# Opening stage of a diffusion-layer kernel: x loaded between the first weight pieces, u prepared in both halves of a period, tile bursts in two parts

## What is computed

```python
def modulation(cvec, w_ada, b_ada):
    mod = jax.nn.silu(cvec) @ w_ada + b_ada          # w_ada: 2048 x 6144
    shift, scale, gate = jnp.split(mod[:, None, :], 3, axis=-1)
    return shift, scale, gate

def mixer_layer(x, shift, scale, gate, w_in, ...):
    u = rmsnorm(x, norm_pre_w) * (1 + scale) + shift
    aq, ak, av, az, mq, mk, mv, mo, mz, mg, ga, gb = split_proj(u, w_in)   # u @ w_in
    ...      # windowed attention, mLSTM, merge
    out = rmsnorm(merged @ w_out, norm_post_w)
    return x + gate * out, ...
```

## Time and profile before

| | before |
| --- | --- |
| median of three runs | 2243.02 us (2242.98 to 2243.2) |
| the profiled execution | 2240.9 us, its span 2239.3 us |
| PE busy | 2123.8 us, 95% of the span |
| DVE, ACT, POOL busy | 868.3, 643.5, 101.5 us |
| PEclk, mean | 0.977 |
| L1377, the products behind the start stage | 66% of the chain that ended last |

### The profile page before, as it was taken

One profiled execution on the slowest core, in us unless ns is written; L12 is line 12 of the kernel. 1 busy time (PEld: TensorE's weight loads), 2 busy tenths in 40 slices (PEclk: granted clock), 3 DMA queues, 4 the chain that ended last, 5 costly groups with the idle time before them and its releaser, 6 DMA issues.

```text
span 2239.3 us, 34071 instructions
## 1 busy us (share of the span) xinstructions
PE 2123.8 (95%) x13450; PEld 1973.3 (88%) x13450; DVE 868.3 (39%) x1666; ACT 643.5 (29%) x1046; POOL 101.5 (5%) x184
## 2 busy tenths in 40 slices
PE   3889999999999999999999999999999899989995
PEld 0459999999999999999999989999999899967774
DVE  4775755432224223222322234343434433342223
ACT  4763111223223323332232222222222422221221
POOL 2001000000000000000000000000000100000000
PEclk7999999999999999999999999999999999999998
DMA  6874656542233234223422335353434534313223
GB/s 247 274 234 123 205 174 173 176 120 75 84 113 88 75 90 119 76 75 90 120 75 76 112 93 138 100 137 100 134 103 107 167 121 122 122 57 122 75 75 131
DMA packets 295166, 274.00 MB, mean 122 GB/s; under 512 B 17920, under 2 KB 243960, under 8 KB 292640
## 3 DMA queue, kind: packets, MB, share of 16 engines
q1 hardware_dynamic: 282416, 218.21, 34.0%
q0 software_dynamic: 12656, 54.40, 6.5%
HBM read 232.65 MB, written 39.92 MB: 122 GB/s over the span
## 4 chain that ended last, share of the span: by engine, by line
PE 90%; DVE 4%; issue 2%; DMA 2%; ACT 1%; SPq 1%; DVEq 0%; POOL 0%; POOLq 0%; ACTq 0%
PE bank L1377 66%; PE bank L1601 9%; PE bank L1466 2%; PE bank L1292 2%; PE bank L1348 2%; PE bank L1516 2%; PE bank L1331 1%; PE bank L1507 1%; PE bank L1518 1%; PE bank L1439 1%; DMA Y<-in_x_prompt_dram 1%; DVE XL L1249 1%; DVE WL L862 1%; DVE XL L1223 0%; PE bank L1421 0%
## 5 line engine op out<-in xcount | busy, mean ns | idle before, releaser
L1377 PE MATMUL bank<-XH,WH 128*128 128x320 f32 x3392 | 790.2, 314 | 20.2 <-POOL WORK L548 7.9
L1377 PE MATMUL bank<-XL,WH 128*128 128x320 f32 x3392 | 774.9, 310 | 0.0
L1377 PE MATMUL bank<-XH,WL 128*128 128x320 f32 x3392 | 774.7, 310 | 0.0
L844 DVE TENSOR_TENSOR WL<-RAW,WH 128x1024 fp32r<-128x1024 f32 x244 | 298.8, 1225 | 998.8 <-ACT WH L618 998.1
L618 ACT ACTIVATE WH<-RAW 128x1024 fp32r<-128x1024 f32 x244 | 258.2, 1059 | 1197.1 <-PE bank L1377 1026.5
L1377 PEld LDWEIGHTS bank<-XH,WH 128*128 128x128 f32 x3392 | 566.7, 189 | 29.7 <-issue 20.4
L1377 PEld LDWEIGHTS bank<-XL,WH 128*128 128x128 f32 x3392 | 569.6, 189 | 0.0
L1377 PEld LDWEIGHTS bank<-XH,WL 128*128 128x128 f32 x3392 | 569.0, 188 | 0.0
L1601 PE MATMUL bank<-WH,XH 128*128 128x512 f32 x320 | 130.7, 408 | 13.9 <-ACT WORK L818 5.9
L1601 PE MATMUL bank<-WH,XL 128*128 128x512 f32 x320 | 126.7, 396 | 0.0
L1601 PE MATMUL bank<-WL,XH 128*128 128x512 f32 x320 | 126.6, 396 | 0.0
(11 more groups left out here) (198 smaller groups left out, 1515.9 us busy)
## 6 DMA issues: line engine op xcount, KB each, us to landing
RAW<-in_w_in_dram SPq DMA_DIRECT2D x180, 512.0 KB, 4.9
proj_dram<-OUTS POOLq DMA_DIRECT2D x92, 320.0 KB, 3.9
WORK<-in_w_ada_dram SPq DMA_DIRECT2D x54, 512.0 KB, 4.1
RAW<-in_w_ada_dram SPq DMA_DIRECT2D x42, 512.0 KB, 4.9
RAW<-in_w_out_dram SPq DMA_DIRECT2D x32, 512.0 KB, 3.7
WORK<-proj_dram SPq DMA_DIRECT2D x20, 640.0 KB, 4.7
WORK<-proj_dram POOLq DMA_DIRECT2D x32, 320.0 KB, 3.8
RAW<-in_w_proj_a_dram SPq DMA_DIRECT2D x16, 512.0 KB, 3.9
```

Of the source, the lines that this page charges most:

```text
L844: V.tensor_tensor(WL[:, gs % 2, :], RAW[:, gs % 4, :], WH[:, gs % 2, :].bitcast(F32), ALU.subtract).then_inc(lo_done, 1)
L1377: ins = pe.matmul(banks[n][:, 0:HALF_TOK], w[:, k, :], x[:, k0 + k, n * HALF_TOK:(n + 1) * HALF_TOK], start=(first and k == 0 and wi == 0) ...
```

## The change

Three edits, all in the start stage:

1. **x between the first pieces.** SP issues piece g, then block g of x, for g = 0 to 4. Each block has a semaphore of its own. ACT squares block g right behind hi(g). DVE makes the mean ahead of lo(6) and scales one block ahead of each of lo(8) to lo(12).
2. **u over both halves.** `start_u(k)` puts the modulation of a chunk at a4, a6, b0 and b2, and so the splits at a5, a7, b1 and b3. The transposes move one piece later on PE and ACT (behind q = 3 to 7), and the copy out waits for the splits that it needs rather than for all four.
3. **Bursts in two parts.** `START_PE` is a list of its own for PE: a burst's first k-block, then the first ada piece of the next group, then the second k-block. `START_DONE[g]` is the place of piece g in PE's count of used pieces, and every wait on `start_used` goes by it. The last three bursts stay whole.

```diff
+START_PE = []
+for _g, (_kind, _j, _q) in enumerate(START):
+    if _kind == "tiles":
+        START_PE += [(_g, 0), (_g, 1)]
+    elif _q == 0 and _g and START[_g - 1][0] == "tiles":
+        START_PE.insert(len(START_PE) - 1, (_g, None))
+    else:
+        START_PE.append((_g, None))
+START_DONE = {}
+for _g, _part in START_PE:
+    if _part != 0:
+        START_DONE[_g] = len(START_DONE) + 1
...
 def start_w_free(g):
 
-    return max((p for p in range(g) if start_w(p) == start_w(g)), default=-1) + 1
+    return max((START_DONE[p] for p in range(g) if start_w(p) == start_w(g)), default=0)
...
+def start_u(k):
+
+    c, i = divmod(k, 4)
+    return start_at("ada", 2 * c + 2, 4 + 2 * i) if i < 2 else start_at("ada", 2 * c + 3, 2 * i - 4)
...
-            for g in range(4):
-                start_load(g)
             for b in range(5):
+                start_load(b)
                 src = x_sample[0, b * P:(b + 1) * P, :] if b < NB else x_prompt[0]
-                sp.dma_start(XT[:, b, :], src).then_inc(x_in, 16)
-            for g in range(4, N_START):
+                sp.dma_start(XT[:, b, :], src).then_inc(x_in[b], 16)
+            for g in range(5, N_START):
                 start_load(g)
...
                 if c:
-                    act.wait_ge(u_lo, 4 * c)
+                    act.wait_ge(u_lo, 4 * c - 3 + min(f, 3))
...
-                if g == 4:
-                    for b in range(5):
-                        act.wait_ge(x_in, 16 * 5)
-                        if b:
-                            act.wait_ge(sq_done, b)
-                        nc.scalar.activation(SQ, XT[:, b, :], ACT.Square, accum_out=SS[:, b:b + 1]).then_inc(sq_done, 1)
...
                 start_hi_part(g)
+                if g < 5:
+                    act.wait_ge(x_in[g], 16)
+                    if g:
+                        act.wait_ge(sq_done, g)
+                    nc.scalar.activation(SQ, XT[:, g, :], ACT.Square, accum_out=SS[:, g:g + 1]).then_inc(sq_done, 1)
                 for c in range(4):
                     for f in range(5):
-                        if g == start_at("ada", 2 * c + 1, 2 + f) + 2:
+                        if g == start_at("ada", 2 * c + 1, 3 + f) + 2:
                             transposed_x(c, f)
                     for i in range(4):
-                        if c < 3 and g == start_at("ada", 2 * c + 2, 4 + i):
+                        if c < 3 and g == start_u(4 * c + i):
                             modulate(c, i)
...
-                if g == 4:
+                if g == 6:
                     dve.wait_ge(sq_done, 5)
                     V.tensor_scalar(SS[:, :], SS[:, :], 1.0 / D, EPS, ALU.mult, ALU.add).then_inc(ms_done, 1)
-                if g == 5:
+                if 8 <= g < 13:
                     dve.wait_ge(rstd_done, 1)
-                    for b in range(5):
-                        V.tensor_scalar(XT[:, b, :], XT[:, b, :], RSTD[:, b:b + 1], None, ALU.mult).then_inc(xn_done, 1)
+                    b = g - 8
+                    V.tensor_scalar(XT[:, b, :], XT[:, b, :], RSTD[:, b:b + 1], None, ALU.mult).then_inc(xn_done, 1)
...
                 for k in range(12):
-                    if g == start_at("ada", 2 * (k // 4) + 2, 4 + k % 4) + 1:
+                    if g == start_u(k) + 1:
                         split_u(k)
...
-            def start_tiles(g, m):
+            def start_tiles(g, m, k):
...
-                if kt < KT - 1:
+                if k == 1 and kt < KT - 1:
                     ins.then_inc(start_used, 1)
 
             pe.wait_ge(cs_done, 1)
-            for g in range(N_START):
+            for g, part in START_PE:
                 kind, j, q = START[g]
                 if kind == "ada":
                     mod_piece(g, j, q)
                     if q == 1 and j:
                         mod_columns(j - 1)
-                    if j % 2 and 2 <= q < 7:
-                        transposed_x(j // 2, q - 2)
+                    if j % 2 and q >= 3:
+                        transposed_x(j // 2, q - 3)
                 else:
-                    start_tiles(g, j)
+                    start_tiles(g, j, part)
```

More of the change, by code:

```diff
@@ L62, in start_w_free @@
 def start_w_free(g):
-    return max((p for p in range(g) if start_w(p) == start_w(g)), default=-1) + 1
+    return max((START_DONE[p] for p in range(g) if start_w(p) == start_w(g)), default=0)
 def start_raw_count(g):
     return sum(16 if START[p][0] == "ada" else 32 for p in range(g % START_RAW, g + 1, START_RAW))
-WIDE_FREE = max(p for p in range(N_START) if start_w(p) >= 2) + 1
+WIDE_FREE = max(START_DONE[p] for p in range(N_START) if start_w(p) >= 2)
+def start_u(k):
+    c, i = divmod(k, 4)
+    return start_at("ada", 2 * c + 2, 4 + 2 * i) if i < 2 else start_at("ada", 2 * c + 3, 2 * i - 4)
 C_IDENT, C_TRIF, C_TRIB, C_SEL, C_PERM, C_BAND, C_COS, C_SIN, C_END = 0, 128, 256, 384, 392, 520, 2056, 2568, 3080
@@ L266, in hybrid_layer @@
         XT = OR
-        rows_in, const_in, x_in, aconst_in = sem("rows_in"), sem("const_in"), sem("x_in"), sem("aconst_in")
+        rows_in, const_in, x_in, aconst_in = sem("rows_in"), sem("const_in"), [sem(f"x_in{b}") for b in range(5)], sem("aconst_in")
         m0_in, mnull = sem("m0_in"), sem("mnull")
@@ L865, in mod_row @@
             def mod_row(j):
-                dve.wait_ge(start_used, start_at("ada", j, 7) + 1)
+                dve.wait_ge(start_used, START_DONE[start_at("ada", j, 7)])
                 if j:
@@ L1333, in mod_piece @@
                 ins.then_inc(start_used, 1)
-            def start_tiles(g, m):
+            def start_tiles(g, m, k):
                 pe.wait_ge(start_lo, g + 1)
                 wh, wl = start_wh[start_w(g)], start_wl[start_w(g)]
-                for k in range(2):
-                    kt = 2 * m + k
-                    if m == 5 and k == 1:
-                        mod_columns(7)
-                    pe.wait_ge(u_lo, kt + 1)
-                    for i in range(3):
-                        cs = slice(384 * k + P * i, 384 * k + P * i + P)
-                        for wi, (w, x) in enumerate(((wh, XH), (wh, XL), (wl, XH))):
-                            for n in range(2):
-                                ins = pe.matmul(bank[2 * i + n][:, 0:HALF_TOK], w[:, cs],
-                                                x[:, kt, n * HALF_TOK:(n + 1) * HALF_TOK],
-                                                start=(kt == 0 and wi == 0), stop=(kt == KT - 1 and wi == 2))
-                        if kt == KT - 1:
-                            ins.then_inc(tiles_done, 1)
-                if kt < KT - 1:
+                kt = 2 * m + k
+                if m == 5 and k == 1:
+                    mod_columns(7)
+                pe.wait_ge(u_lo, kt + 1)
+                for i in range(3):
+                    cs = slice(384 * k + P * i, 384 * k + P * i + P)
+                    for wi, (w, x) in enumerate(((wh, XH), (wh, XL), (wl, XH))):
+                        for n in range(2):
+                            ins = pe.matmul(bank[2 * i + n][:, 0:HALF_TOK], w[:, cs],
+                                            x[:, kt, n * HALF_TOK:(n + 1) * HALF_TOK],
+                                            start=(kt == 0 and wi == 0), stop=(kt == KT - 1 and wi == 2))
+                    if kt == KT - 1:
+                        ins.then_inc(tiles_done, 1)
+                if k == 1 and kt < KT - 1:
                     ins.then_inc(start_used, 1)
             pe.wait_ge(cs_done, 1)
-            for g in range(N_START):
+            for g, part in START_PE:
                 kind, j, q = START[g]
```

## The result

The changed kernel takes 2227.4 us (median of four runs, 2225.42 to 2228.63) against 2243.0 of the kernel before: a ratio of 0.9932, 95% interval 0.992 to 0.9944, 15.6 us faster. I had forecast 2233.5 with a range from 2228.5.

The account below looks back on a forecast made before the run. PE, busy 95% of the span, was taken as the bound, so the start stage had to end sooner: 9.0 + 0.95 + 1.7 - 2.55 + 0.4 = 9.5 us, from 2240.9 to 2231.4 profiled, median 2233.5; range 2228.5 to 2237.5.

Parts of the forecast that it names:

- x between the pieces: Opening: last block of x in at 25.65, lo(12) ending at 47.5 instead of 56.5, 9.0 us gained.
- The price of a scaling, 1.74: DVE in the opening: each of five scalings of x counted at 1.74 us, 8.7 together.
- Behind lo(12) the order is as before: Opening after lo(12): hi steps and copies alternate on ACT as before, so the mod_columns move by the same 9.0 us.
- Second halves: The two second halves: 1.27 us less on DVE, 0.4 lost to T1's later place, 0.85 gained twice, 1.7 us.
- First halves, the stall: The three first halves: PE stalls 0.85 us ahead of b4 behind the fourth split, 2.55 us lost in all.
- The gaps ahead of T0 get a little shorter but stay, so I keep this loss, less 0.4 in all: First halves: slow-clock losses of 1.06, 1.25 and 1.44 us stay, only 0.4 us of them gained.
- The tail: Last stretch, from 170.7 us: last three bursts whole, order kept, no gain; unchanged at 17.8 us.
- The half burst: PE in the start stage: half a burst estimated at about 2.65 us, from a first half's 17.60 less its other work.
- the third: Rival, first halves: PE stays at 1.2 GHz, up to 16.5 us more each; 2250 for one, 2283 for three; 3%.
- The first rival: Start stage: the stalls vanish, PE full throughout and no clock loss; 26 us gained, 2217; 5%.

Follow-up runs that it names:

- x only: The kernel before with the first edit alone (x between the pieces, squares and scalings spread): 2236.62 us, ratio 0.997.
- the three kernels of the table: Bursts only and the kernel before with eight or three filler matmuls in PE's gaps: 2242.63, 2255.09 and 2238.83 us.
- x and shift: The kernel before with the first edit and, of the second, only the transposes one piece later: 2233.99 us, ratio 0.9959.
- bursts only: The kernel before with the third edit alone, bursts in two parts: 2242.63 us, ratio 1.0002.
- u only: The kernel before with the second edit alone, u over both halves and transposes one piece later: 2233.88 us, ratio 0.9965.
- filler runs: The kernel before with eight or three matmuls nobody reads in each of PE's gaps ahead of a5, a6, a7 and T0: 2255.09 and 2238.83 us.
- eight-matmul filler: The kernel before with eight matmuls nobody reads in each of PE's gaps ahead of a5, a6, a7 and T0: 2255.09 us, ratio 1.0064.
- filler, three: The kernel before with three matmuls nobody reads in each of PE's gaps ahead of a5, a6, a7 and T0: 2238.83 us, ratio 0.998.
- x and u: The kernel before with the first and second edit, bursts whole: 2225.22 us, ratio 0.9924.
- u and bursts: The kernel before with the second and third edit, x loaded, squared and scaled as before: 2236.4 us, ratio 0.9972.
- late memset: The changed kernel with POOL clearing its accumulator only after all five blocks of x are scaled: 2223.32 us, ratio 0.9916.

## Why the prediction was too small

By its own steps, profiled execution against profiled execution, where the last burst starts 14.2 us earlier instead of 9.5:

- **x between the pieces**: the chain was right. x came in at 25.64 (25.65), lo(12) ended 8.7 us earlier (9.0). The price of a scaling, 1.74, was the mean of a long one and four short ones; in the changed kernel they took 4.52 and four times 1.27, 9.6 together against 8.77. That cost the forecast little, but it hid a gain that was there to be had.
- **"Behind lo(12) the order is as before"** was wrong, since the transposes stand one piece later, and the figure built on it came out near by luck. With the order really kept (x only) the second columns stand at 59.75, 6.9 us earlier and not 9.0 (7.8 against the 67.6 of the three kernels of the table that keep the old opening and the old place of the transposes): PE was at the slow clock there, for which I had nothing in the sum and up to 1 us in the range. The shift of the transposes won 1.9 back (x and shift, 57.84), and in the trace of the changed kernel the clock came back early besides: 56.88, 9.73 us earlier. Together with the stretch behind it (10.91 us from the columns to the burst, forecast some 11.1) the first burst came 10.85 us earlier instead of 9.95: 0.9 us of the miss, which is no more than the spread of the clock's return between single executions.
- **Second halves**: forecast 0.85 less, measured 0.93 and 0.91. Right, with its parts: bursts only has the 0.4 longer (0.37), u only has the 1.27 less (19.35 - 18.07 = 1.28).
- **First halves, the stall** ahead of b4: forecast 0.85, there with 0.72; the whole first half at full clock is 17.17 against the 16.66 of the filler runs, so 0.5 of it counts at the end: 1.55 us in three places instead of 2.55, 1.0 of the miss.
- **"The gaps ahead of T0 get a little shorter but stay, so I keep this loss, less 0.4 in all"**: this is the step that failed. The gaps did stay, three of four of them, but the loss didn't stay with them. I had the loss of before nearly right (1.06 + 1.25 + 1.44 = 3.75 by the windows, 3.3 by the filler runs) and kept 3.35 of it. In the changed kernel 17.41, 17.21 and 17.16 leave some 0.25 in the first burst and nothing in the others: 3.1 us of the miss, less the 0.4 by which I had the loss of before too large. The cause is shown: the edit that keeps the clock in the first halves is the second (u only, PEclk 0.99 to 1.00), not the third (bursts only, 0.92 to 0.93) and not the first (x only, 0.89 to 0.91), nor the shift of the transposes (x and shift, first halves of 18.1 to 18.2); and filling the pauses does the same with the order untouched.
- **The tail**: 17.8 before, 17.9 after, as said.
- **The half burst**: the working that I gave for 2.65 comes to 2.95. Measured it is 2.71 (85.20 to 87.91), and nothing in the sum hung on it.

These make 0.9 + 0.1 + 1.0 + 3.1 - 0.4 = 4.7, the 14.2 against 9.5. Another 1.3 us of the profiled difference (15.5) lies behind the start stage, where the two kernels have the same instructions. From the last burst to the end all traces but that of the eight-matmul filler take between 2066.6 and 2069.9 us (before 2068.6, changed 2067.4), so it lies within the spread of single executions.

Of the rivals, the third pointed the wrong way. I took "HAM oscillation — how this bites in real kernels" of the Trainium skill, "TensorE: Matmul & The Clock Gate", as a warning against parted bursts. The runs agree with the rule itself: what pauses too much loses its clock (x only), what is filled keeps it (filler, three). The page's case is a PE that waits for DMAs; here pauses of 1.0 to 1.3 us behind DVE were enough. The runs say that the parting of the bursts mattered neither way for it, and that the spread of the splits, which closes one of four pauses, was the application of the rule here. I read it for the part that looked chopped and not for the part that removed waits. The first rival (stalls vanish) came true for the clock alone, not for DVE's share: the wait of ACT for T1's place is still there with 3.77 us in the changed kernel:

```profile
91.74 1.06 ACT L661 ACTIVATE WH<-RAW 128x1024 fp32r<-128x1024 f32 x1 [3.77 <-PE bank L1365]
```

## What to carry to other kernels

Where PE waits in short pauses, look at the clock behind them: the pauses cost twice, and an edit that removes even one of four can win back the clock for work that it doesn't touch. Take the loss out of the sum as a term of its own with its own chance, and don't carry it over by habit; a few filler matmuls in the gaps measure it (3.3 us here) with nothing else changed. An edit in three parts should be run in parts: here the third cost some 1.9 us in the stage (x and u against the changed kernel, u only against u and bursts) and only the first two earned. Look past the stage that an edit touches, too: most of what the eight filler matmuls lost was lost where they don't stand. Open the merged rows of a timeline before using their mean as a price.

## What the runs showed of the hardware

A scaling of 128 x 2048 float32 on DVE, SBUF to SBUF with one tensor operand, took 1.27 us by itself and 4.52 us beside a memset of 128 x 4096 on POOL that began 0.07 us ahead of it; with the memset moved away it took 1.29. The lo steps, with two tensor operands, did not suffer: with the late memset, which ran from 44.25 to 47.78, two of them took the usual 2.34 from 44.12 on. The Trainium skill, "SBUF — State Buffer", section "Who interferes with whom", says that VectorE in a two-port mode and GpSimd take a shared pair of ports as a lock, and whoever comes second is blocked for the whole instruction: 3.5 us of memset and the scaling's own 1.2 make 4.7 from the memset's start, and the row ends at 36.67, 4.6 after it. That this scaling was in such a mode, no run shows. POOL's root of 128 x 5 took 2.03 us from 30.08 in the changed kernel, where a lo step had begun at 29.83, and 1.20 from 35.15 in the kernel before, where the next lo step began at 35.77; what held it was not tested.

And 36 matmuls whose results nobody reads took 3.9 us off the median (filler, three), since they stood in pauses and the work behind them then ran at 2.4 GHz.
